# RWKV chunk recurrence, four slots: left half of the Gram product copied by ScalarE, level-one dx in another bank, k copies moved, one output unit loaded in halves

## Chip, cores and metric

The kernel runs on one core of a Trainium2 chip. The metric is device time in microseconds, median of the runs. Of a profiled execution the span is given, from its first instruction to its last.

## What is computed

Two transformer stacks after each other, in float32, for 256 tokens of width 1024: a short convolution mixer, an RWKV-7 mixer, a sparse attention, a forgetting attention, and an MLP of width 4096 behind each of them. Only the recurrence of the RWKV mixer is touched:

```python
def frame_step(state, inp):
    r_t, w_t, k_t, v_t, a_t, b_t = inp
    sa = jnp.einsum('bhvk,bhk->bhv', state, a_t)
    state = (state * w_t[:, :, None, :]
             + sa[..., None] * b_t[:, :, None, :]
             + v_t[..., None] * k_t[:, :, None, :])
    y_t = jnp.einsum('bhvk,bhk->bhv', state, r_t)
    return state, y_t
```

It runs over 256 tokens for 16 heads of 64. In the mixer it is followed by a group norm, a bonus term r*k*v, a gate, and the output projection `rw_w_o`.

## The kernel before

**Chunks and slots.** The 256 tokens are cut in 4 chunks of 64, and the 16 heads in 4 slots of 4 heads (two tiles of 128 rows, each with 2 heads; these two are the halves q = 0 and 1). In a chunk the recurrence is solved by matrices: the Gram product of b with (a, r) gives a strictly triangular 64x64 matrix, whose inverse I - N is built by doubling, in levels 0 to 5. The name for the inverse is `inv_t`, for its transpose `inv_x`. From the inverse, a chain over the 4 chunks gives right-hand side, u, the state and y.

**Steps.** A list, written out by hand, holds the steps of a slot in an order that all engines follow: gram 0, gram 1, tok 0, tok 1, then for each level 1 to 5: t1 0, t1 1, dx 0, dx 1. Between them stand the chain steps rhs, u, sy of the slot before. In slots 1 to 3 the start is: gram 0, rhs (chunk 0), gram 1, u, sy, tok 0, tok 1, t1 0, t1 1 (level 1), rhs (chunk 1), dx 0, u, dx 1, t1 0 (level 2), sy, t1 1, dx 0, dx 1. An engine runs its part of each step in that order and waits by semaphores.

**TensorE** (line 2642 for all products of 64x64): gram 0 writes b x (a, r) into banks `acc[0]`, `acc[1]` (per chunk 64 columns with a, 64 with r) and v, turned, into `un`; gram 1 writes k x (a, r) into `acc[2]`, `acc[3]`; tok turns b and k into `un`; t1 is `n_m` times `inv_x` into the first half of `acc[q]`; dx is t1 times the inverse into the second half of `acc[2 + q]`. In slot 0 products of the value projection are spread between the steps (line 2252 onwards, tile `side`), in slots 2 and 3 a product for the bonus (line 2618) and one for the variance (line 2627).

**VectorE**, gram q: reads the raw product twice, with the level-0 mask (line 1992, to `inv_t`) and the level-1 mask (1993, to `n_m`), adds the identity (1994), writes the product under both masks to `nb_t` (1995, 512 columns; the left, a, columns serve later levels, the right, r, columns y), and transposes (1996). tok q: `nk_t` from `acc[2 + q]` under both masks (2000). dx q: adds dx to the late columns of `inv_t` (2005) and transposes (2008). u: copies y of the chunk before (1980, 1982). sy: the state (2020, 2022). In slot 0 it also prepares mixer inputs (1882 to 1889).

**ScalarE**: gram q copies v (1281), t1 q copies t1 (1287) and in level 1 also the turned b and k (1290); rhs and u are copied at 1293 and 1301. At tok 1 it makes the two decay exponentials for the next slot (`wkv_build`, 1140 and 1141). In slot 0 it computes inverse norms behind step 0 (1169 to 1174) and splits weights (882) behind step 1.

**GpSimd**: for levels 2 to 5 multiplies the left columns of `nb_t` by the level's mask into `n_m` (line 817). Between levels it builds b and k (`build_bk`) and a and r (`build_ar`) of the next slot, and behind them the gate's products.

**SyncE** loads weight units of 1 MB into four stage buffers. Two of these hold, in the RWKV part, arrays of slot 0 and 2 (`v_tok2`, `inv_t2` in the first 4 KB of a partition, `bk_tok2` in the second), so the load of unit `BESIDE_SLOT[0] + NSTAGE`, the third unit of the output projection, waits until the four y of slot 0 are done (line 633).

## Time and profile before

| | us |
|---|---|
| median of three runs | 1351.57 |
| lowest and highest run | 1350.92, 1353.13 |
| span of the profiled execution | 1350.7 |
| TensorE busy in it | 1303.9 (97%) |
| VectorE busy | 948.4 (70%) |
| ScalarE busy | 701.1 (52%) |
| GpSimd busy | 128.3 (9%) |

The slots run from 427.0 to 527.7 us of the span, a last round of chain steps with rows of the output projection to 552.9. A line of a timeline gives start and duration in us, engine, line, operation, tile written <- tiles read, shapes, how many instructions, and in brackets how long the engine was idle before and what ended that. PE is TensorE, PEld its weight load, DVE VectorE, ACT ScalarE, POOL GpSimd, SPq SyncE's queue. "Issue" is idle time for which the profile shows nothing that was awaited. The instruction queue (q8) brings the engines' instructions in pieces of 16 KB.

### The profile page before, as it was taken

To read this page: it belongs to the slowest core of one execution; us is meant where nothing else is said; L and a number is where in the kernel's file an instruction comes from. 1 tells how busy PE (TensorE), PEld (TensorE's weight loads), DVE (VectorE), ACT (ScalarE), POOL (GpSimd) and SP (SyncE) were. 2 spreads that over 40 slices of the span, in tenths; PEclk is the share of its full clock that TensorE was granted. 3 is DMA by queue.
4 is the path that set the end of the run, shared out by engine and by line. 5 is a ranking of instruction groups with operands and counts; after the bars stand their busy time and mean duration, and the time that the engine had idled before them with its cause. 6 is when DMAs were issued, how large, how long until landed. Compare 5 with 4: busy or idle time off the path is not lost. (4 is left out here: it accounts for less than half of the span.)

```text
span 1350.7 us, 24951 instructions
## 1 busy us (share of the span) xinstructions
PE 1303.9 (97%) x10507; PEld 1130.7 (84%) x10507; DVE 948.4 (70%) x1433; ACT 701.1 (52%) x1211; POOL 128.3 (9%) x133
## 2 busy tenths in 40 slices
PE   4999999999999999999999999999999999999997
PEld 2998888997899887788888887888888998888886
DVE  1887788976768776685556888666657677756655
ACT  2534544434467455564444648654445566644443
POOL 0000000010200864100000142000000021000000
PEclk9999999999999999999999999999999999999999
DMA  9997899995341012356665532465565544565561
GB/s 363 373 366 236 302 350 381 356 344 161 110 156 64 4 35 97 98 178 196 188 192 177 176 121 74 150 203 192 187 196 160 170 143 126 172 188 192 183 197 51
DMA packets 177559, 256.90 MB, mean 190 GB/s; under 512 B 10472, under 2 KB 122536, under 8 KB 177448
## 3 DMA queue, kind: packets, MB, share of 16 engines
q1 hardware_dynamic: 177448, 255.31, 57.0%
q8 instruction: 83, 1.36, 0.4%
q14 instruction: 28, 0.23, 0.0%
HBM read 254.25 MB, written 1.05 MB: 189 GB/s over the span
## 5 line engine op out<-in xcount | busy, mean ns | idle before, releaser
L1507 DVE TENSOR_TENSOR w_lo<-stage,w_hi 128x1024 fp32r<-128x1024 f32 (+1 forms) x372 | 447.3, 1238 | 160.4 <-ACT w_hi L882 160.0
L882 ACT ACTIVATE w_hi<-stage 128x1024 fp32r<-128x1024 f32 (+1 forms) x378 | 379.9, 1049 | 211.7 <-PE acc L2311 191.9
L2309 PE MATMUL acc<-w_hi,z_hi 128*128 128x512 f32 x640 | 252.7, 395 | 1.6 <-DVE z_lo L1956 1.6
L2311 PE MATMUL acc<-w_hi,z_lo 128*128 128x512 f32 x640 | 249.4, 390 | 0.0
L2310 PE MATMUL acc<-w_lo,z_hi 128*128 128x512 f32 x640 | 249.2, 389 | 0.0
L2252 PE MATMUL un<-h_both,w_hi 128*128 128x256 f32 x736 | 214.9, 292 | 1.8 <-POOL w_lo L853 1.1
L2253 PE MATMUL un<-h_both,w_hi 128*128 128x256 f32 x736 | 208.8, 284 | 0.0
L2254 PE MATMUL un<-h_both,w_lo 128*128 128x256 f32 x736 | 208.8, 284 | 0.0
L2252 PEld LDWEIGHTS un<-h_both,w_hi 128*128 128x128 f32 x736 | 141.6, 192 | 9.5 <-issue 5.4
L2309 PEld LDWEIGHTS acc<-w_hi,z_hi 128*128 128x128 f32 x640 | 120.1, 188 | 27.8 <-issue 3.9
L2253 PEld LDWEIGHTS un<-h_both,w_hi 128*128 128x128 f32 x736 | 141.7, 193 | 1.2 <-issue 0.7
L2254 PEld LDWEIGHTS un<-h_both,w_lo 128*128 128x128 f32 x736 | 141.7, 193 | 0.0
L2311 PEld LDWEIGHTS acc<-w_hi,z_lo 128*128 128x128 f32 x640 | 120.1, 188 | 25.4
L2310 PEld LDWEIGHTS acc<-w_lo,z_hi 128*128 128x128 f32 x640 | 120.2, 188 | 23.4
L2290 PE MATMUL un<-h_both,w_hi 128*128 128x512 f32 x384 | 121.2, 397 | 0.4 <-DVE w_lo L1507 0.4
L2290 PE MATMUL side<-h_both,w_hi 128*128 128x512 f32 x384 | 120.8, 396 | 0.4
L2293 PEld LDWEIGHTS side<-h_both,w_lo 128*128 128x128 f32 x384 | 72.1, 188 | 17.0
L2293 PEld LDWEIGHTS un<-h_both,w_lo 128*128 128x128 f32 x384 | 72.1, 188 | 16.9
L2293 PE MATMUL un<-h_both,w_lo 128*128 128x256 f32 x384 | 75.5, 278 | 0.0
L2293 PE MATMUL side<-h_both,w_lo 128*128 128x256 f32 x384 | 75.5, 278 | 0.0
L1789 DVE SCALAR_TENSOR_TENSOR ada_sum<-ada_buf,small,ada_sum 128x1024 f32<-128x1024 f32 x49 | 62.8, 1282 | 1.0
L2290 PEld LDWEIGHTS un<-h_both,w_hi 128*128 128x128 f32 x384 | 59.1, 189 | 1.7 <-DVE w_lo L1507 0.6
(393 smaller groups left out, 1885.1 us busy)
## 6 DMA issues: line engine op xcount, KB each, us to landing
stage<-in_mlp_w SPq DMA_DIRECT2D x64, 1024.0 KB
ada_buf<-in_ada_w SPq DMA_DIRECT2D x48, 1024.0 KB, 11.1
stage<-in_w_up SPq DMA_DIRECT2D x32, 1024.0 KB
stage<-in_w_down SPq DMA_DIRECT2D x32, 1024.0 KB
stage<-in_conv_w_in SPq DMA_DIRECT2D x12, 1024.0 KB
stage<-in_rw_w_rkv SPq DMA_DIRECT2D x12, 1024.0 KB
stage<-in_w_in_a SPq DMA_DIRECT2D x8, 1024.0 KB
stage<-in_w_kv_b SPq DMA_DIRECT2D x8, 1024.0 KB
```

Source lines behind the costliest of these rows:

```text
L882: A_(w_hi[u % 2][:, half, 0:n], stage[u % NSTAGE][:, half, 0:n], ACT.Copy).then_inc(hi_made, 1)
L1507: V.tensor_tensor(w_lo[u % 2][:, half, 0:n], stage[u % NSTAGE][:, half, 0:n], w_hi[u % 2][:, half, 0:n].bitcast(F32), ALU.subtract).then_i ...
L1789: V.scalar_tensor_tensor(out=to[:], in0=rows, scalar=by, in1=to[:], op0=ALU.mult, op1=ALU.add).then_inc(ada_weighed, 1)
L2252: MM(out, hi_l, hi_r, start=start, stop=False, skip_group_check=True)
L2253: MM(out, hi_l, lo_r, start=False, stop=False, skip_group_check=True)
L2254: return MM(out, lo_l, hi_r, start=False, stop=stop, skip_group_check=True)
L2290: MM(pair[:, m, :, :], wh[:, kt, c], h_both[:, kt, :, :], start=(kt == 0), stop=False, skip_group_check=True)
L2293: ins = MM(pair[:, m, 0, :], wl[:, kt, c], h_hi[:, kt, :], start=False, stop=(kt == KT - 1), skip_group_check=True)
L2309: MM(y, z_hi[:, kt, q], wh[:, i, :], start=(first and kt == 0), stop=False, skip_group_check=True)
L2310: MM(y, z_hi[:, kt, q], wl[:, i, :], start=False, stop=False, skip_group_check=True)
L2311: ins = MM(y, z_lo[:, kt, q], wh[:, i, :], start=False, stop=(last and kt == KT - 1), skip_group_check=True)
```

## The change

SyncE loads the third unit of the output projection as two halves: the first when it loaded the whole, the second when two more y are done. ScalarE's gram steps copy the left columns of the raw Gram product into `nb_t`, unmasked, first those of `acc[1]`, then, when VectorE has read `acc[0]`, those of `acc[0]`; the two copies of v come behind the second. VectorE masks the right columns only, and waits ahead of that for both copies. GpSimd's level-2 multiplication waits for the copies, and not for VectorE's transpose; in slots 1 and 2 its builds for the next slot come one level later. ScalarE's exponentials move from tok 1 to behind t1 1 of level 1. VectorE's masked copies of the k product move from tok to behind dx of level 1; dx of level 1 goes into the second half of `acc[q]`, and the wait for the k copy goes to dx of level 2. The other edits renumber semaphores, since ScalarE signals five times a slot where it signalled four times.

```diff
--- before.py
+++ after.py
@@ -633,6 +633,13 @@
                     sp.wait_ge(sem("y_done"), CHUNKS)
                 if u == BESIDE_SLOT[1] + NSTAGE:
                     sp.wait_ge(sem("y_done"), CHUNKS * 3)
+                if u == BESIDE_SLOT[0] + NSTAGE:
+                    (_, _, src), = units[u]
+                    for half in range(2):
+                        if half:
+                            sp.wait_ge(sem("y_done"), CHUNKS + 2)
+                        sp.dma_start(stage_wide[u % NSTAGE][:, 2 * half:2 * half + 2, :], src[:, 2 * half:2 * half + 2, :]).then_inc(landed[u % NSTAGE], 16)
+                    return
                 for lo, hi, src in units[u]:
                     sp.dma_start(stage_wide[u % NSTAGE] if u in wide else stage[u % NSTAGE][:, :, lo:hi], src).then_inc(landed[u % NSTAGE], 32 // len(units[u]))
 
@@ -811,14 +818,14 @@
                 for j in WKV_LEVELS[1:]:
                     for q in range(2):
                         if j == 2:
-                            pool.wait_ge(inv_ready, 12 * s + q + 1)
+                            pool.wait_ge(tok_out, 5 * s + 2)
                         else:
                             pool.wait_ge(t1_done, 10 * s + 2 * (j - 3) + q + 1)
                         G.tensor_tensor(n_m[(j - 1) % 2][:, q, :, :], nb_t[s % 2][:, q, :, 0:CHUNK],
                                         level_t[:, j, :].unsqueeze(1).to_broadcast([P, CHUNKS, CHUNK]), ALU.mult).then_inc(nm_ready, 1)
-                    if j == (2 if s else 4) and s + 1 < SLOTS:
+                    if j == (3 if s else 4) and s + 1 < SLOTS:
                         build_bk(s + 1)
-                    if j == (3 if s else 5) and s + 1 < SLOTS:
+                    if j == (4 if s else 5) and s + 1 < SLOTS:
                         build_ar(s + 1)
                     if j == 4 and s >= 2:
                         group_weigh(s - 2)
@@ -1276,18 +1283,25 @@
             for slot in range(SLOTS + 1):
                 for n, (step, s, j, q) in enumerate(wkv_steps(slot)):
                     if step == "gram":
-                        act.wait_ge(v_done, s + 1)
-                        act.wait_ge(lo_made, 2 * (BESIDE_SLOT[0] + 1))
-                        A_(v_tok[SLOT_SET[s]][:, q, :, :], half_bank(un[q], 1), ACT.Copy).then_inc(tok_out, 1)
-                    elif step == "tok":
-                        if q == 1 and s + 1 < SLOTS:
-                            wkv_build(s + 1)
+                        if q == 0:
+                            act.wait_ge(g_done, s + 1)
+                            act.wait_ge(lo_made, 2 * (BESIDE_SLOT[0] + 1))
+                        else:
+                            act.wait_ge(lak_ready, 3 * s + 1)
+                        A_(nb_t[s % 2][:, 1 - q, :, 0:CHUNK], bank4(acc[1 - q])[:, :, 0:CHUNK], ACT.Copy).then_inc(tok_out, 1)
+                        if q:
+                            act.wait_ge(v_done, s + 1)
+                            for m in range(2):
+                                ins = A_(v_tok[SLOT_SET[s]][:, m, :, :], half_bank(un[m], 1), ACT.Copy)
+                            ins.then_inc(tok_out, 1)
                     elif step == "t1":
                         act.wait_ge(t1_done, 10 * s + 2 * (j - 1) + q + 1)
                         A_(t1[:, q, :, :], half_bank(acc[q], 0), ACT.Copy).then_inc(t1_out, 1)
                         if j == 1:
                             act.wait_ge(tok_done, s + 1)
                             A_(bk_tok[SLOT_SET[s]][:, q, :, :, :].rearrange("p b c s -> p (b c s)"), flat(un[q]), ACT.Copy).then_inc(tok_out, 1)
+                            if q == 1 and s + 1 < SLOTS:
+                                wkv_build(s + 1)
                     elif step == "rhs":
                         act.wait_ge(rhs_done, CHUNKS * s + j + 1)
                         A_(wkv_rhs[:], two_pairs(stat_ps), ACT.Copy).then_inc(rhs_out, 1)
@@ -1988,25 +2002,32 @@
                     if step == "gram":
 
                         dve.wait_ge(g_done, s + 1)
+                        if q:
+                            dve.wait_ge(tok_out, 5 * s + 1)
                         raw_n = acc[q][:, :, :].rearrange("p a s -> p (a s)").rearrange("p (c q) -> p c q", c=CHUNKS)
                         V.tensor_tensor(xt, raw_n[:, :, 0:CHUNK], bc4(level_t[:, 0, :], CHUNKS), ALU.mult)
-                        link(V.tensor_tensor(n_m[0][:, q, :, :], raw_n[:, :, 0:CHUNK], bc4(level_t[:, 1, :], CHUNKS), ALU.mult))
+                        ins = V.tensor_tensor(n_m[0][:, q, :, :], raw_n[:, :, 0:CHUNK], bc4(level_t[:, 1, :], CHUNKS), ALU.mult)
+                        if q == 0:
+                            ins.then_inc(lak_ready, 1)
+                            dve.wait_ge(lak_ready, 3 * s + 1)
+                        else:
+                            link(ins)
                         V.tensor_tensor(xt, xt, bc4(eye, CHUNKS), ALU.add)
-                        link(V.tensor_tensor(nb_t[s % 2][:, q, :, :], raw_n, bc4(c_("masks"), CHUNKS), ALU.mult))
+                        dve.wait_ge(tok_out, 5 * s + 2)
+                        link(V.tensor_tensor(nb_t[s % 2][:, q, :, CHUNK:2 * CHUNK], raw_n[:, :, CHUNK:2 * CHUNK], bc4(c_("masks")[:, CHUNK:2 * CHUNK], CHUNKS), ALU.mult))
                         V.transpose(in_line(xn), in_line(xt)).then_inc(inv_ready, 1)
-                    elif step == "tok":
-
-                        dve.wait_ge(gk_done, s + 1)
-                        V.tensor_tensor(nk_t[s % 2][:, q, :, :], bank4(acc[2 + q]), bc4(c_("masks"), CHUNKS), ALU.mult).then_inc(lak_ready, 1)
                     elif step == "dx":
 
                         dve.wait_ge(dx_done, 10 * s + 2 * (j - 1) + q + 1)
                         x_ = late(in_line(xt), j)
-                        ins = V.tensor_tensor(x_, late(flat(acc[2 + q])[:, 2 * P:4 * P], j), x_, ALU.add)
+                        ins = V.tensor_tensor(x_, late(flat(acc[q if j == 1 else 2 + q])[:, 2 * P:4 * P], j), x_, ALU.add)
                         if j < WKV_LEVELS[-1]:
                             link(ins)
                             ins = V.transpose(in_line(xn), in_line(xt))
                         ins.then_inc(inv_ready, 1)
+                        if j == 1:
+                            dve.wait_ge(gk_done, s + 1)
+                            V.tensor_tensor(nk_t[s % 2][:, q, :, :], bank4(acc[2 + q]), bc4(c_("masks"), CHUNKS), ALU.mult).then_inc(lak_ready, 1)
                     elif step == "sy":
                         c = j
                         if c < CHUNKS - 1:
...
                     elif step == "dx":
-                        if j == 1:
-                            pe.wait_ge(lak_ready, 2 * s + q + 1)
+                        if j == 2:
+                            pe.wait_ge(lak_ready, 3 * s + q + 2)
                         pe.wait_ge(t1_out, 10 * s + 2 * (j - 1) + q + 1)
                         for c in range(CHUNKS):
-                            ins = by_head(late(half_bank(acc[2 + q], 1)[:, c, :], j), t1[:, q, c, :], late(xt[:, c, :], j))
+                            ins = by_head(late(half_bank(acc[q if j == 1 else 2 + q], 1)[:, c, :], j), t1[:, q, c, :], late(xt[:, c, :], j))
                         ins.then_inc(dx_done, 1)
...
```

## Rows read from the trace of the kernel before

**Rows 1.** Stretches: us, busy (instructions) of PE, PEld, DVE, ACT, POOL; clock, DMA, GB/s.

```profile
...
426.96:455.02 28.06, 27.36 (x574) 25.25 (x574) 23.39 (x43) 17.53 (x36) 14.09 (x14) 1.00 0.01 3
455.02:478.26 23.24, 21.05 (x712) 19.96 (x709) 18.32 (x51) 12.21 (x33) 18.38 (x19) 1.00 0.03 5
478.26:503.07 24.81, 22.76 (x722) 21.31 (x719) 18.67 (x52) 14.43 (x38) 14.18 (x15) 1.00 0.12 46
503.07:527.69 24.62, 22.73 (x721) 21.23 (x717) 19.40 (x55) 12.75 (x35) 13.42 (x15) 1.00 0.05 10
...
```

**Rows 2.** Waits, 426 to 553 us: total, times, longest.

```profile
...
PE acc L2642 <- DVE inv_x L1996: 2.5, 3, 1.5
...
PE un L2642 <- issue: 1.5, 1, 1.5
...
```

**Rows 3.** Timeline, TensorE, slot 1: start, duration, line, operation [idle before <- releaser].

```profile
...
462.18 0.68 PE L2642 MATMUL acc<-inv_x,n_m 64*64 64x64 f32 x16 [1.50 <-DVE inv_x L1996]
...
464.01 0.45 PE L2642 MATMUL side<-wkv_rhs,inv_t 64*64 64x64 f32 x8
...
465.46 0.45 PE L2642 MATMUL side<-v_tok,bk_tok 64*64 64x64 f32 x8
...
```

**Rows 4.** Timeline, TensorE, slots 2 and 3.

```profile
...
483.92 0.40 PE L2642 MATMUL un<-const,b_fm 64*64 64x64 f32 x12 [1.51 <-issue]
...
485.50 0.22 PE L2642 MATMUL side<-v_tok,nk_t 64*64 64x64 f32 x1
...
487.02 1.13 PE L2618 MATMUL un<-rw,const 128*128 128x256 f32 x4
...
509.49 0.68 PE L2642 MATMUL acc<-inv_x,n_m 64*64 64x64 f32 x16 [0.80 <-DVE inv_x L1996]
...
```

**Rows 5.** Timeline, TensorE, slot 0.

```profile
...
439.44 1.15 PE L2642 MATMUL acc<-inv_x,n_m 64*64 64x64 f32 x32
...
449.69 1.34 PE L2642 MATMUL acc<-inv_x,n_m 64*64 64x64 f32 x32 [0.42 <-DVE inv_x L2008]
...
```

**Rows 6.** DMA by queue, 467 to 475 us: packets, MB, share.

```profile
...
q8 instruction: 3, 0.05, 2.6%
...
```

**Rows 7.** DMA by queue, 481 to 482 us.

```profile
...
q8 instruction: 1, 0.02, 6.2%
...
```

**Rows 8.** DMA in 40 slices of 475 to 481 us.

```profile
...
GB/s 0 0 0 0 0 0 0 0 0 0 0 0 0 0 0 0 0 0 0 68 27 14 82 41 14 164 410 396 396 410 423 396 396 423 437 396 396 410 423 396
...
```

**Rows 9.** Timeline, VectorE, slot 2.

```profile
...
479.86 0.41 DVE L1993 TENSOR_TENSOR n_m<-acc,const 128x256 f32<-128x256 f32 x1
480.31 0.42 DVE L1994 TENSOR_TENSOR inv_t<-inv_t,const 128x256 f32<-128x256 f32 x1
480.65 0.68 DVE L1995 TENSOR_TENSOR nb_t<-acc,const 128x512 f32<-128x512 f32 x1
481.37 0.45 DVE L1996 STREAM_TRANSPOSE inv_x<-inv_t 128x256 f32<-128x256 f32 x1
...
484.26 1.28 DVE L2000 TENSOR_TENSOR nk_t<-acc,const 128x512 f32<-128x512 f32 x2
...
```

**Rows 10.** Timeline, VectorE, slot 3.

```profile
...
505.04 1.13 DVE L1994 TENSOR_TENSOR inv_t<-inv_t,const 128x256 f32<-128x256 f32 x1
...
```

**Rows 11.** Timeline, ScalarE, slot 0.

```profile
...
430.86 1.08 ACT L1174 ACTIVATE ka_mix<-rw,small,vecT 128x256 f32<-128x256 f32 x2
...
```

**Rows 12.** Timeline, VectorE, slot 1.

```profile
...
464.05 0.29 DVE L2005 TENSOR_TENSOR inv_t<-acc,inv_t 128x128 f32<-128x128 f32 x1 [0.37 <-PE acc L2642]
...
464.95 0.46 DVE L1982 COPY tmp<-side 64x64 f32<-64x64 f32 x2
...
```

**Rows 13.** Timeline, VectorE, slot 0.

```profile
...
444.89 0.29 DVE L2005 TENSOR_TENSOR inv_t<-acc,inv_t 128x128 f32<-128x128 f32 x1 [0.67 <-PE acc L2642]
...
```

**Rows 14.** Timeline, ScalarE, slot 1.

```profile
...
458.23 0.62 ACT L1140 ACTIVATE w_cum<-rw 128x512 f32<-128x512 f32 x1
...
463.67 0.28 ACT L1293 ACTIVATE wkv_rhs<-side 128x128 f32<-128x128 f32 x1
...
```

More of the change, by code:

```diff
@@ L2613, in group_step @@
                     if j < 2:
-                        pe.wait_ge(tok_out, 4 * (j + 2) + 4)
+                        pe.wait_ge(tok_out, 5 * (j + 2) + 5)
                     pe.wait_ge(bonus_ready, j)
@@ L2621, in group_step @@
                 if j < 2:
-                    pe.wait_ge(tok_out, 4 * (j + 2) + 3)
+                    pe.wait_ge(tok_out, 5 * (j + 2) + 4)
                 if j:
@@ L2661, in _ @@
                                 pe.wait_ge(t1_out, 10 * s)
-                            pe.wait_ge(tok_out, 4 * s)
+                            pe.wait_ge(tok_out, 5 * s)
                             if s == SLOTS - 1:
@@ L2683, in _ @@
                         if q == 0:
-                            pe.wait_ge(tok_out, 4 * s + 2)
+                            pe.wait_ge(tok_out, 5 * s + 3)
                         for c in range(CHUNKS):
@@ L2711, in _ @@
                                 pe.wait_ge(inv_ready, 12 * s + 12)
-                                pe.wait_ge(tok_out, 4 * s + 4)
-                                pe.wait_ge(lak_ready, 2 * s + 2)
+                                pe.wait_ge(tok_out, 5 * s + 5)
+                                pe.wait_ge(lak_ready, 3 * s + 3)
                                 pe.wait_ge(un_free, freed(V_RKV + 11))
```

## The prediction, made before the changed kernel had run

> **What bounds the kernel now.** I read the table of stretches first. The part that the change touches is the RWKV recurrence, four slots of 28.06, 23.24, 24.81 and 24.62 us [rows 1], and TensorE is busy for 91 to 98% of each. So almost no gain is to be had by making another engine cheaper: what can be won is the sum of TensorE's idle pieces. The table of who waited for whom, for the slots and the output projection behind them, says what those are [rows 2]: 2.5 us in three waits for the transposed inverse of the Gram step (VectorE's line 1996), one of them 1.5 us, and 1.5 us in one piece of "issue", in which nothing in the program was awaited. Behind the slots TensorE runs on almost without a gap into projection and MLP, so that what a slot gains or loses arrives at the end one for one.
>
> Next the timelines. In slot 1 the second half's first product (t1, level 1) starts after 1.50 us of idle, at 462.18 [rows 3]: VectorE makes five operations for each of the two halves, one after the other, and both halves and the next chain step hang on it. In slot 3 the same wait shows as 0.80 us at 509.49 [rows 4]. In slot 2 it is hidden behind the "issue" hole at 482.4 to 483.92 [rows 4]. In slot 0 TensorE has the value projection to do and comes to that product only at 439.44 [rows 5], long after VectorE.
>
> The hole has a neighbour in the DMA view. From 467 to 475 us three 16 KB fetches of the instruction queue went out, some 3.6 us apart [rows 6]. The next one is in 481 to 482 [rows 7], in the last part of the 1 MB load of an output unit, which is issued when the fourth y of slot 0 is done and runs at full rate from 478.7 to about 481.5 [rows 8]. TensorE then ran dry until 483.92.
>
> **The Gram step on VectorE.** Before, one half costs: two reads of the raw product (the second 0.45 from start to start, with its wait), the addition of the identity 0.34, the mask over all 512 columns 0.72 to the transpose, and the transpose itself [rows 9]. The change halves the mask; the 256-column read beside it lasts 0.41, or 0.45 with its wait, so 0.27 is saved for a half, 0.54 for a slot, and not the whole 0.68, since the masked right part stays. Two new waits eat of it. ScalarE copies the left part, and may read a bank only while VectorE does not; in the first half VectorE waits for a copy that starts once it has read twice. A copy of 256 columns from PSUM takes ScalarE what its copy of v takes, which I put at 0.38 by the same shape; VectorE's identity addition of 0.34 hides most of it. In slot 1 I leave 0.1 over. In slot 2 ScalarE's copy of the first right-hand side comes before it in its queue, and I leave 0.25. In slot 3 VectorE's addition is itself stretched to 1.13 [rows 10], which covers the copy wholly. So the second t1 comes earlier by 0.45 (slot 1), 0.3 (slot 2) and 0.5 (slot 3).
>
> In slot 0 the order on ScalarE is bad: behind its first copy stand three passes and two more activations of the inverse norms, whose last begin at 430.86 and end at 431.94 [rows 11]. The second copy comes after them, so VectorE waits from about 429.3 to 432.3 and ends its Gram step near 435 instead of 432.7. I cost this at nothing: the product that needs it starts at 439.44 [rows 5], which leaves more than 4 us. If that cover were gone it would be 2.5 us.
>
> **The masked copies of the k Gram, moved.** Two of them take 1.28 in slot 2 [rows 9]. They stood before the first dx; there VectorE has been idle afterwards (0.37 in slot 1 [rows 12]), so they hid. Now one stands behind each dx of level 1, in front of the copies of y, the next dx and the state. Slot by slot, each 0.64:
> Slot 1: dx of the first half would be read at about 463.6 instead of 464.05, its transpose ends at 464.25, then comes the k copy until 464.9 and the copies of y until 465.6. Before, the first of y's last two copies began at 464.95 [rows 12], ended by 465.4, and TensorE's step began at 465.46 [rows 3] directly behind it. So that step is now at about 465.75: the 0.45 won turns into 0.3 lost.
> Slots 2 and 3: the bonus product of 1.13 us [rows 4] stands in TensorE's queue between the first dx and the step that wants y, so the copies have room and the gain stays.
> Slot 0: VectorE goes on with mixer work after each dx, and reads the level-2 dx at 444.89 after 0.67 of idle [rows 13]. 1.28 more, less 0.67, is 0.6 late, and TensorE, which waited 0.42 for just this chain at 449.69 [rows 5], waits 0.6 more. VectorE has no idle time between the two. I take +0.6; bounds 0 and +1.28.
>
> **The decay exponentials on ScalarE, moved.** Two activations of 0.62 [rows 14] now come behind the second copy of b and k, right in front of the copy of the second right-hand side (463.67 in slot 1), for which TensorE's next step at 464.01 waits [rows 3, 14]. In slot 1 that step comes at about 464.45 (0.45 late); VectorE's k copy above runs in the same time, so the two delays overlap and slot 1 stays at +0.3; bounds -0.45 (none of it bites) and +0.6. In slot 2 the bonus product again covers it but for 0.1. In slot 0 ScalarE has idle time there. Slot 3 has none to make.
>
> **GpSimd.** Its level-2 multiplications no longer wait for VectorE's transpose and start about 1 us earlier in slots 1 and 2; the build of b and k for the next slot goes behind level 3, and that of a and r behind level 4. Level 3 can be multiplied as soon as the second t1 is over. The queue then stands waiting for the exponentials until about 464.3, and the build ends 1.5 us later than now, but the next slot starts at 478.26 [rows 1], and level 4 is multiplied by 468.3, wanted near 472. Nothing on the path.
> What can cost is that two engines meet: VectorE's addition of the identity took 0.42 in slot 2, with GpSimd idle, and 1.13 in slot 3, with GpSimd at work on the gate [rows 9, 10], and the level-2 multiplications now fall on just such VectorE operations. I take +0.1 for all slots, bounds 0 and 0.7 (1.13 less 0.42) for each of three slots. The Trainium skill, SBUF — State Buffer, section "SBUF: two separate sides", says that a VectorE operation with two SBUF inputs and a GpSimd operation that reads SBUF exclude each other for the whole instruction. By that rule the stretch would be up to one GpSimd operation for each meeting; the row of slot 3 agrees, 0.71 longer; the sum by it would be 2.1 instead of 0.1 at most.
>
> **Level one's dx in its own bank.** Same 32 products, another address. It lets dx start without the k copy. TensorE didn't wait for that copy in any slot: its queue order set the start. Worth 0, and the waits at level 2 are long met (the first k copy of slot 1 ends at 464.9, that dx is after 466).
>
> **The output unit in halves.** SyncE issues 0.5 MB when it issued 1 MB, and 0.5 MB when two more y are done, in slot 2 near 492. Nobody wants the unit before the projection, 55 us later, and the queue's next load waits for y of slot 3 anyway. So it costs nothing. At the rate shown, some 400 GB/s from 478.7 [rows 8], the first half is through at about 480.1 instead of 481.5. If the fetch, due near 478.4, has waited for the load, it comes 1.4 us earlier, about the length of the hole, 1.51 us [rows 4]. I take the hole as gone. VectorE is then the one that is late: its Gram step ended near 483.9, a state update before the k copies at 484.26 [rows 9], and would end at 483.6, the second t1 is through by 484.2 and the next chain product begins there instead of at 485.50: -1.3; the bonus product, at 487.02 [rows 4] because it waited for ScalarE's copies of b and k, brings 0.2 more and ScalarE's exponentials cost 0.1: slot 2 -1.4, bounds 0 (hole stays) and -1.8. The second half could delay a fetch near 493 to 495 by at most its own 1.4 us; a delay of some 3 us made a hole of 1.5, so this one should make at most 0.3, which is inside the bounds.
>
> **Sum.** Slot 0 +0.6, slot 1 +0.3, slot 2 -1.4, slot 3 -0.5, meetings +0.1: -0.9 us. The profiled span is 1350.7, so 1349.8; the median of the three timed runs, 1351.57, lies 0.87 over that span, so 1350.7 us.
>
> **Rivals.** *The hole stays*, because the fetch and the load are neighbours and not cause and effect. For it: no row shows the fetch waiting, only that it is late. Against: the three fetches before it keep their distance, and it comes with the load's end. Slot 2 then gives 0 and the sum is +0.5: 1352.1 us. The Trainium skill, DMA: Bandwidth & Descriptors, section "Queues, rings and completion order", speaks for this rival: each DMA engine takes turns between queues packet by packet, so a fetch would be held up by one packet and not by a megabyte. By that rule the time would be this rival's; the trace so far disagrees, with a fetch that came only in the load's last microsecond.
> *All of it is cover*: the k copies and exponentials fall into idle time in slots 0 and 1 too. Slot 0 at 0, slot 1 -0.45, slot 2 -1.7, slot 3 -0.5: -2.65, 1348.9 us. For it: VectorE is busy only 75 to 83% of each slot [rows 1]. Against: the idle time is not in front of the two steps named.
> *VectorE becomes the bound* (the slower side): after level 1 both halves alternate through VectorE, and the 1.28 us of k copies come out on the path in each of four slots, 5.1 in all, from the point at which VectorE's idle time before the level-2 dx (0.67 in slot 0, about 0.35 in the others) is less than the copies. Less 1.2 of Gram gains, less 1.0 for the hole with the old rest: +2.9, 1354.5 us. Against: bonus products in slots 2 and 3 give VectorE 0.5 to 0.9 of idle just there.
>
> **How the numbers follow.** Forecast 0.60, hole stays 0.18, all cover 0.14, VectorE the bound 0.05, else 0.03. A measurement of this kernel can tell about 0.2%, 2.7 us, from no change: below 1348.9 is faster, above 1354.3 slower. Forecast and hole-stays lie well inside; half of all-cover, and some of the scatter of the forecast (the runs of before span 2.2 us), goes to faster: 0.14. VectorE-the-bound and scatter give slower 0.07, and 0.79 is left. The range takes in both neighbours and the scatter around them: 1348.3 to 1353.6.
>
> **What would show it.** Right: no "issue" idle of TensorE near 482; an instruction fetch between 479 and 480.5; slot 2 shorter by 1.2 to 1.6, slot 3 by 0.5, slot 1 longer by 0.3 with TensorE waiting for the copies of y (line 1982's place) instead of the transpose, slot 0 longer by 0.6 with a wait near 450. Wrong: a hole of 1 us or more anywhere in slots 1 to 3, slot 0 unchanged, or VectorE additions of 1 us in slots 1 and 2.

## The result and the profile after

The changed kernel takes 1353.9 us, median of 14 runs (1353.25 to 1355.35), where the kernel before, on the same chip, takes 1351.49 (14 runs, 1350.65 to 1354.65). The ratio is 1.0017, 95% interval 1.0010 to 1.0024: 2.4 us slower, just under the 0.2% that I had set as what can be told, with an interval that leaves no change out. The forecast was 1350.7, with a range up to 1353.6: a gain of 0.8 us where 2.4 were lost, wrong by 3.2 and 0.3 above the range.

The table of stretches, cut at the Gram starts of the kernel after, answers to [rows 1]. The last stretch runs here to the first row of the output projection; the same stretch of before is the first line.

```profile
...
503.07:532.49 29.42, 27.35 (x792) 24.78 (x789) 21.44 (x59) 15.35 (x42) 18.14 (x19) 1.00 0.21 69
...
```

```profile
...
427.44:456.62 29.18, 27.87 (x573) 25.55 (x574) 24.55 (x43) 18.14 (x38) 15.18 (x15) 1.00 0.01 3
456.62:480.87 24.25, 20.85 (x713) 19.85 (x709) 18.59 (x52) 12.88 (x35) 16.76 (x18) 1.00 0.02 4
480.87:505.51 24.64, 22.92 (x720) 21.28 (x718) 18.94 (x52) 15.04 (x40) 14.14 (x15) 1.00 0.15 46
505.51:534.70 29.19, 27.41 (x795) 24.86 (x791) 20.93 (x59) 16.06 (x44) 18.10 (x19) 1.00 0.21 70
...
```

The second number of a line is its length. Against 28.06, 23.24, 24.81 and 29.42 that is +1.12, +1.01, -0.17 and -0.23: +1.73 us in the slots. Another 0.48 us lies before them (the first Gram product starts at 427.44, not at 426.96), where no instruction was changed. That is not the change's: in the profiles of the experiments below this start lies anywhere from 426.86 to 429.44, and at 426.86 and 426.87 in e3 and e4, which differ from the kernel after only behind it. So 1.73 us is what the change did in the slots; the rest of the 2.4 is of the size by which runs of one kernel differ.

The table of who waited for whom shows how the idle time of TensorE has changed hands. [Rows 2] had 2.5 us in three waits for the transposed inverse of the Gram step and 1.5 in a single piece of "issue". Of after, the rows for TensorE and the longest new ones of others:

```profile
...
PE acc L2663 <- DVE inv_x L2026: 2.6, 7, 0.7
DVE nb_t L2017 <- ACT nb_t L1291: 2.4, 1, 2.4
...
ACT nb_t L1291 <- DVE n_m L2009: 1.5, 1, 1.5
...
PE side L2663 <- ACT wkv_u L1315: 1.4, 1, 1.4
...
PE side L2663 <- ACT wkv_rhs L1307: 1.2, 2, 1.0
```

Line 2026 is the transpose behind a dx (2008 of before): TensorE now waits for that seven times, 2.6 us. It waits 1.4 and 1.2 us for ScalarE's copies of u and of the right-hand side, for which the same table of before has no row. The big old waits are gone; new ones stand at other producers. The timeline of TensorE after, the pieces of it that answer to [rows 3 to 5]: two in slot 0, three in slot 1, three in slot 2 (the middle one is the chain product of [rows 4], without idle time) and one in slot 3.

```profile
...
447.39 1.34 PE L2663 MATMUL acc<-inv_x,n_m 64*64 64x64 f32 x32 [0.63 <-DVE inv_x L2026]
...
451.30 0.93 PE L2663 MATMUL acc<-inv_x,n_m 64*64 64x64 f32 x18 [0.54 <-DVE inv_x L2026]
...
461.48 0.39 PE L2663 MATMUL side<-wkv_u,bk_tok 64*64 64x64 f32 x6 [1.39 <-ACT wkv_u L1315]
...
463.61 0.68 PE L2663 MATMUL acc<-inv_x,n_m 64*64 64x64 f32 x16 [0.29 <-DVE inv_x L2018]
...
466.47 0.45 PE L2663 MATMUL side<-wkv_rhs,inv_t 64*64 64x64 f32 x8 [1.03 <-ACT wkv_rhs L1307]
...
485.22 0.40 PE L2663 MATMUL un<-const,b_fm 64*64 64x64 f32 x12 [0.26 <-issue]
...
486.81 0.22 PE L2663 MATMUL side<-v_tok,nk_t 64*64 64x64 f32 x1
...
499.40 0.68 PE L2663 MATMUL acc<-inv_x,n_m 64*64 64x64 f32 x16 [0.72 <-DVE inv_x L2026]
...
511.71 0.68 PE L2663 MATMUL acc<-inv_x,n_m 64*64 64x64 f32 x16 [0.40 <-DVE inv_x L2018]
...
```

**Slot 1** shows the exchange best. The second t1, which had waited 1.50 [rows 3], starts at 463.61: 6.99 us behind the slot's start, before 7.16. So 0.17 is won where 0.45 was forecast. The rest of that wait has moved in front of the u step at 461.48. ScalarE's timeline says why:

```profile
...
460.32 0.38 ACT L1291 ACTIVATE nb_t<-acc 128x256 f32<-128x256 f32 x1 [1.49 <-DVE n_m L2009]
460.60 0.66 ACT L1295 ACTIVATE v_tok<-un 128x256 f32<-128x256 f32 x2
461.13 0.30 ACT L1315 ACTIVATE wkv_u<-side 128x128 f32<-128x128 f32 x1
...
464.62 0.59 ACT L1302 ACTIVATE bk_tok<-un 128x512 f32<-128x512 f32 x1
465.10 0.63 ACT L1147 ACTIVATE w_cum<-rw 128x512 f32<-128x512 f32 x1
465.62 0.63 ACT L1148 ACTIVATE w_inv<-rw 128x512 f32<-128x512 f32 x1
466.14 0.28 ACT L1307 ACTIVATE wkv_rhs<-side 128x128 f32<-128x128 f32 x1
...
```

The second copy of a left half may start only when VectorE has read that bank twice; ScalarE stands 1.49 us for it, and behind it in its queue are the two copies of v and the copy of u that TensorE wants. Then the exponentials, 465.10 to 466.2, stand in front of the copy of the right-hand side, and TensorE waits 1.03. That step comes 9.85 us behind the slot's start; before it was 464.01 - 455.02 = 8.99 [rows 3]. It is 0.86 late against the kernel before, not 0.45.

**Slot 2.** The "issue" piece is 0.26 instead of 1.51 [rows 4], and the next chain product starts at 486.81, 5.94 behind the slot's start, where it was 485.50 - 478.26 = 7.24: 1.30 earlier, as forecast. But at the slot's end only 0.17 of that is left. The fences show VectorE's split of an output unit in slot 2 (its product w_lo, the rest of a weight), before and then after, and GpSimd beside it in the kernel after.

```profile
...
494.75 1.30 DVE L1507 TENSOR_TENSOR w_lo<-stage,w_hi 128x1024 fp32r<-128x1024 f32 x1 [0.33 <-ACT w_hi L882]
...
```

```profile
...
496.33 2.21 DVE L1521 TENSOR_TENSOR w_lo<-stage,w_hi 128x1024 fp32r<-128x1024 f32 x1 [0.32 <-ACT w_hi L889]
...
```

```profile
...
496.19 1.27 POOL L801 TENSOR_TENSOR rw<-tmp,rw 128x512 f32<-128x512 f32 x1 [0.15 <-POOL ar L783]
497.42 2.39 POOL L824 TENSOR_TENSOR n_m<-nb_t,const 128x256 f32<-128x256 f32 x2
...
```

GpSimd's weighing of a group runs 496.19 to 497.46 and VectorE's split is issued 0.14 us after its start. The split ends at 498.54, which is the end of the weighing and 1.1 us more: it looks as if it had waited for it. GpSimd's next two multiplications, issued at 497.42, take 2.39 us, and 1.42 elsewhere (440.70), as if they in turn had waited for the split. The next inverse is late by it, and TensorE waits 0.72 at 499.40. Before, the weighing was at 492.95, through before the split began.

**Slot 0.** VectorE's timeline after, first the wait of 2.36 us for the second left copy, which I had foreseen (about 3 us), then what stands behind the level-one dx; below it the same three mixer lines of before.

```profile
...
432.25 0.42 DVE L2017 TENSOR_TENSOR nb_t<-acc,const 128x256 f32<-128x256 f32 x1 [2.36 <-ACT nb_t L1291]
...
443.81 0.65 DVE L2030 TENSOR_TENSOR nk_t<-acc,const 128x512 f32<-128x512 f32 x1
444.38 1.01 DVE L1896 TENSOR_TENSOR tmp<-tmp,ss_inv 128x512 f32<-128x512 f32 x1
445.43 1.10 DVE L1897 SCALAR_TENSOR_TENSOR tmp<-tmp 128x512 f32<-128x512 f32 x1
446.56 0.29 DVE L2023 TENSOR_TENSOR inv_t<-acc,inv_t 128x128 f32<-128x128 f32 x1
...
447.91 1.52 DVE L1899 SCALAR_TENSOR_TENSOR rw<-rw,tmp 128x512 f32<-128x512 f32 x1
...
```

```profile
...
442.85 0.65 DVE L1882 TENSOR_TENSOR tmp<-tmp,ss_inv 128x512 f32<-128x512 f32 x1
443.53 0.69 DVE L1883 SCALAR_TENSOR_TENSOR tmp<-tmp 128x512 f32<-128x512 f32 x1
...
446.24 1.04 DVE L1885 SCALAR_TENSOR_TENSOR rw<-rw,tmp 128x512 f32<-128x512 f32 x1
...
```

The k copies don't only take their own 1.2 us. They push the mixer operations from 442.85 to 444.38, which is 1.05 us later behind the slot's start, where GpSimd is at work from 444.12 on, and the three lines take 3.63 instead of 2.38.

### The profile page after: what moved, and what is told of

Same layout as the page of the kernel before. It is cut to its first block and busy times, and to the rows that moved or that the text cites. A ratio compares the mean times of both kernels' runs of the same rounds, so it can differ in the third digit from the quotient of the medians.

```text
span 1351.8 us, 24960 instructions
## 1 busy us (share of the span) xinstructions
PE 1303.7 (96%) x10507; PEld 1130.7 (84%) x10507; DVE 949.7 (70%) x1433; ACT 703.6 (52%) x1219; POOL 127.7 (9%) x133
## 3 DMA queue, kind: packets, MB, share of 16 engines
HBM read 254.25 MB, written 1.05 MB: 189 GB/s over the span
```

## The experiments

Lengths are us from Gram start to Gram start, the fourth to the first projection row; "sum" also has the 20.4 us of the projection's rows, which are the same in all. They are the fine measure here, since the scatter of whole runs is as large as what is looked for. A median is of 11 runs, or of as many as stand in brackets behind it. The intervals are of the ratio to the kernel before on the same chip.

| kernel | slot 0 | 1 | 2 | 3 | sum | median | ratio, 95% |
|---|---|---|---|---|---|---|---|
| before | 28.06 | 23.24 | 24.81 | 29.42 | 125.92 | | 1 |
| after | 29.18 | 24.25 | 24.64 | 29.19 | 127.64 | 1353.9 (14) | 1.0010 to 1.0024 |
| e1: before, halves | 28.08 | 23.26 | 23.75 | 29.46 | 124.93 | 1350.7 (11) | 0.9977 to 0.9995 |
| e2: after, whole load | 29.19 | 24.24 | 25.76 | 29.18 | 128.75 | 1354.96 | 1.0013 to 1.0030 |
| e3: after, exponentials back | 29.19 | 23.91 | 24.20 | 29.19 | 126.88 | 1353.8 | 1.0000 to 1.0017 |
| e4: after, builds back | 29.20 | 24.24 | 23.89 | 29.19 | 126.91 | 1353.93 | 1.0003 to 1.0020 |
| e5: after, k copies back | 28.55 | 23.92 | 24.39 | 29.18 | 126.42 | 1352.43 | 1.0000 to 1.0017 |
| e6: all three back | 28.54 | 22.82 | 23.13 | 29.29 | 124.19 | 1350.39 (11) | 0.9977 to 0.9995 |
| e7: e1, k copies moved | 29.18 | 25.38 | 24.43 | 29.46 | 128.82 | 1353.24 | 1.0003 to 1.0021 |
| e8: e1, builds later | 28.04 | 23.75 | 24.32 | 29.46 | 125.94 | 1351.97 | 0.9995 to 1.0013 |
| e9: e6, norms later | 28.00 | 22.82 | 23.54 | 29.14 | 123.88 | 1349.7 (11) | 0.9977 to 0.9995 |
| e10: after, norms later | 29.19 | 24.24 | 24.40 | 29.19 | 127.41 | 1353.88 (10) | 1.0008 to 1.0027 |
| e11: after, weighing cut | 29.20 | 24.23 | 23.77 | 29.19 | 126.77 | 1354.03 (1) | |

**The load in halves, alone and left out.** e1 is the kernel before with only this edit; e2 is the kernel after without it.

```diff
+                if u == BESIDE_SLOT[0] + NSTAGE:
+                    (_, _, src), = units[u]
+                    for half in range(2):
+                        if half:
+                            sp.wait_ge(sem("y_done"), CHUNKS + 2)
+                        sp.dma_start(stage_wide[u % NSTAGE][:, 2 * half:2 * half + 2, :], src[:, 2 * half:2 * half + 2, :]).then_inc(landed[u % NSTAGE], 16)
+                    return
```

> The kernel before with the output unit loaded in halves and nothing else. If the fetch waited for the load: TensorE's issue hole in slot 2 goes from 1.5 us to 0.3 or less, slot 2 goes from 24.8 to about 23.8 us (VectorE's Gram step is next in line there), the total to 1.0 us below before. If fetch and load are only neighbours: hole and total as before.

> The changed kernel with the output unit loaded whole again. If the fetch waited for the load: a hole of 1.5 us in slot 2 and the slot 1.0 to 1.3 us longer than in the changed kernel (24.64). If not: no difference to the changed kernel.

Measured: slot 2 falls by 1.06 in e1 and rises by 1.12 in e2, and no other slot moves. TensorE's timeline, e1 and then e2:

```profile
...
484.52 0.40 PE L2649 MATMUL un<-const,b_fm 64*64 64x64 f32 x12 [0.33 <-issue]
...
```

```profile
...
486.15 0.40 PE L2656 MATMUL un<-const,b_fm 64*64 64x64 f32 x12 [1.37 <-issue]
...
```

And the DMA view, 40 slices and the queue's row: e1, in 482 to 483 us, and e2, in 483 to 484 us. The slice of 655 GB/s in the first, and that of 984 in the second, hold the fetch.

```profile
...
GB/s 82 0 0 0 655 0 0 0 0 0 0 0 0 0 0 0 0 0 0 0 0 0 0 0 0 0 0 0 0 0 0 0 0 0 0 0 0 0 0 0
...
q8 instruction: 1, 0.02, 5.7%
...
```

```profile
...
GB/s 164 410 492 410 246 573 410 246 573 492 82 655 573 82 573 573 164 410 492 410 164 573 410 164 492 410 0 984 328 0 0 164 0 0 0 0 0 0 0 0
...
q8 instruction: 1, 0.02, 6.3%
...
```

In all four kernels the fetch comes with the last bytes of the load that is under way, or up to 0.2 us behind them: at 481.35 and 483.68 behind the whole megabyte (before, e2), at 482.10 and 482.68 behind the half (e1, after). The fetch ahead of it, at about 477.4 in after and 477.3 in e2, is through before the load moves in both. Behind the slot's start that is 3.1 and 3.0 us with the whole load, 2.0 and 1.8 with the half, and the product that ends TensorE's idle piece starts 2.4 to 2.6 us behind the fetch in each of the four. So the load is the cause of the hole, in both kernels, and the rival that they are only neighbours falls. The fetch still waits for the half load; it only has less to wait for. The halves alone are worth 1.0 to 1.1 us.

**Each moved step taken back by itself.** e3 puts ScalarE's exponentials back at the second tok step, e4 GpSimd's two builds back one level, e5 VectorE's k copies back at tok (the dx of level one stays in its own bank in all).

```diff
+                    elif step == "tok":
+                        if q == 1 and s + 1 < SLOTS:
+                            wkv_build(s + 1)
...
-                            if q == 1 and s + 1 < SLOTS:
-                                wkv_build(s + 1)
```

```diff
-                    if j == (3 if s else 4) and s + 1 < SLOTS:
+                    if j == (2 if s else 4) and s + 1 < SLOTS:
                         build_bk(s + 1)
-                    if j == (4 if s else 5) and s + 1 < SLOTS:
+                    if j == (3 if s else 5) and s + 1 < SLOTS:
                         build_ar(s + 1)
```

```diff
+                    elif step == "tok":
+                        dve.wait_ge(gk_done, s + 1)
+                        V.tensor_tensor(nk_t[s % 2][:, q, :, :], bank4(acc[2 + q]), bc4(c_("masks"), CHUNKS), ALU.mult).then_inc(lak_ready, 1)
...
-                        if j == 1:
-                            dve.wait_ge(gk_done, s + 1)
-                            V.tensor_tensor(nk_t[s % 2][:, q, :, :], bank4(acc[2 + q]), bc4(c_("masks"), CHUNKS), ALU.mult).then_inc(lak_ready, 1)
```

> The changed kernel with ScalarE's two decay exponentials back at the tok step. If the queue on ScalarE is the cause of the loss: TensorE's wait of 1.03 us for the copied right-hand side in slot 1 goes, slot 1 goes from 24.25 to about 23.3 us, slot 2 by 0.2, the total by 1.0 to 1.2. If the meetings of GpSimd and VectorE are the cause, GpSimd's builds come 1.3 us earlier and what they meet changes: slot 1 gains less than 0.5 net.

> The changed kernel with GpSimd's builds of b, k and of a, r back behind levels 2 and 3 in slots 1 and 2. If meetings of GpSimd and VectorE are the cause: VectorE's weight split in slot 2 takes 1.3 instead of 2.2 us and slot 2 shortens by 0.9, the split in slot 1 by 0.4, slot 0 stays at 29.2. If ScalarE's queue is the cause: no more than 0.2 in all, and GpSimd now stands waiting for the exponentials with level 3 queued behind it, which would cost a few tenths.

> The changed kernel with VectorE's masked copies of the k product back at the tok step. If the moved k copies make slot 0 longer, by pushing VectorE's mixer work among GpSimd's multiplications: slot 0 from 29.2 back to 28.1 us, VectorE's five mixer operations of level 2 to 4 together from 6.0 back to about 4.7. If the wait of 2.4 us for ScalarE's left copy in slot 0 is what costs: slot 0 stays at 29.2. Slot 1 changes by less than 0.3 either way, since ScalarE's queue holds TensorE there.

Measured: 0.76, 0.73 and 1.22 us come back, 2.71 if added, in different slots: the exponentials in slots 1 and 2 (0.34, 0.44), the builds in slot 2 alone (0.75), the k copies in slot 0 (0.63), slot 1 (0.33) and slot 2 (0.25). Three expectations were missed. The exponentials were expected to give back 0.95 in slot 1. The builds were expected to shorten VectorE's split in slot 1 by 0.4, but it takes 1.64 us in e4 and 1.66 in after, and that slot doesn't move. The k copies were expected to bring slot 0 back to 28.1; it comes to 28.55, and e9 below shows what holds the rest. Their 0.33 in slot 1 is a meeting too: VectorE's split at the slot's start takes 1.76 us in after and 1.44 in e5, and the second t1 comes 6.99 and 6.67 behind the slot's start. In e3 TensorE's wait for the right-hand side in slot 1 is gone, and the wait that lay under it comes out, for the copies of y that now stand behind a k copy:

```profile
...
466.91 0.45 PE L2664 MATMUL side<-v_tok,bk_tok 64*64 64x64 f32 x8 [0.50 <-DVE tmp L1997]
...
```

That is the wait which the forecast gave slot 1, and it shows that two of the moved steps were late for the same TensorE step, one hidden under the other.

**All three back.** e6 has all three edits at once: what is left of the change are the left copies by ScalarE, the Gram order on VectorE, GpSimd's earlier level-2 multiplication, level one's dx in its own bank and the halves.

> The changed kernel with k copies, exponentials and GpSimd's builds all where they were: what is left of the change is the left copy by ScalarE, level one's dx in its own bank, the earlier level-2 multiplication and the load in halves. If moved work is the cause of the loss and the Gram part is sound: slots of 28.1, 22.9, 23.4 and 29.1 (to the first output row), total 1.8 to 2.2 below before. If the left copy itself costs (waits between ScalarE and VectorE): slots 0 and 1 at or above 28.1 and 23.2, total no better than the load in halves alone (1.0 below before by slots).

Measured: 3.45 us less than after, 0.74 more than the three single steps, so they covered for each other. Slots 1 and 2 are the shortest yet, 0.42 and 1.68 under before. The time is 1350.39, ratio 0.9986. The Gram part of the change is sound by the slots: beyond e1 it brings 0.44 in slot 1, 0.62 in slot 2 and 0.17 in slot 3, and costs 0.46 in slot 0 (where 28.1 us had been expected).

**Moved alone.** e7 is e1 with the k copies moved and the dx of level one in its own bank, without ScalarE's copies; e8 is e1 with the builds one level later (the reverse of e4's diff).

> The kernel before, with the load in halves, level one's dx in its own bank and the k copies behind dx; nothing of the Gram part, exponentials or builds. If the moved k copies cost by VectorE's order: slot 0 28.7 to 29.2 instead of 28.08, slot 1 23.9 to 24.1 instead of 23.26 (the copies of y come 0.65 later and TensorE waits for them), slot 2 and 3 unchanged within 0.2. If they only cost together with the other moves: all slots within 0.2 of the load in halves alone.

> The kernel before, with the load in halves, and GpSimd's builds in slots 1 and 2 one level later; nothing else. If meetings of GpSimd and VectorE cost: VectorE's weight split in slot 2 goes from 1.5 to 2.0 us or more and the slot grows by 0.4 to 0.8 over 23.75, slot 1 within 0.4. If GpSimd's order is off the path: slots unchanged within 0.1.

Measured: in e7 slot 0 takes 29.18, which is after's 29.18, so the k copies alone are enough for slot 0's loss, 1.10 us. (Taking them back in e5 returned only 0.63, since the late left copy then comes out from under them.) Slot 2 loses 0.68, where nothing had been expected: TensorE's piece of "issue" there is 0.96 us and in e1 0.33, so that most of the loss is the hole come back, with the load in halves, and not shown to be the k copies'. Slot 1 loses 2.1, but there the granted clock was 0.72 in the mean of 465 to 471 us, and about 1.2 of it is that (below). In e8 the builds cost 0.49 in slot 1 and 0.57 in slot 2, with nothing else changed. VectorE's split took 1.25 and 1.52 us in the two slots of e1; in e8:

```profile
...
470.00 1.80 DVE L1514 TENSOR_TENSOR w_lo<-stage,w_hi 128x1024 fp32r<-128x1024 f32 x1 [0.32 <-ACT w_hi L889]
...
494.07 2.03 DVE L1514 TENSOR_TENSOR w_lo<-stage,w_hi 128x1024 fp32r<-128x1024 f32 x1 [0.33 <-ACT w_hi L889]
...
```

So the loss goes with the stretch of that one operation: 0.55 and 0.51 longer, 0.49 and 0.57 lost.

**The meeting by itself.** e11 is the kernel after, in which GpSimd's weighing of the first normalised group works on 8 of the 256 columns of each block. It leaves the rest of that product out and keeps its signals.

```diff
-                G.tensor_tensor(rw_k[:, t, :], y_wkv[:, t, :], rw_k[:, t, :], ALU.mult).then_inc(weighed, 1)
+                w = 8 if j == 0 else SEQ
+                G.tensor_tensor(rw_k[:, t, 0:w], y_wkv[:, t, 0:w], rw_k[:, t, 0:w], ALU.mult).then_inc(weighed, 1)
```

> The kernel after, with GpSimd's first weighing of a normalised group cut from 256 columns of each block to 8 (its work left out there, its signals kept). Theory (GpSimd's operations on the shared memory stretch VectorE's split of output weights in slot 2, 2.21 us where it takes 1.30 alone): the split starts at 496.3 as before and takes 1.9 us or less, TensorE's wait for inv_x behind it falls from 0.72 to 0.4 us or less and slot 2 from 24.64 to 24.3. Rival (the split takes 2.2 us because of ScalarE or the arriving load beside it): it stays at 2.2, and so do the wait and the slot.

VectorE and GpSimd in slot 2 of e11:

```profile
...
497.75 1.23 DVE L1522 TENSOR_TENSOR w_lo<-stage,w_hi 128x1024 fp32r<-128x1024 f32 x1 [0.33 <-ACT w_hi L890]
...
```

```profile
...
497.62 0.22 POOL L802 TENSOR_TENSOR rw<-tmp,rw 128x16 f32<-128x16 f32 x1 [0.15 <-POOL ar L783]
497.80 2.46 POOL L825 TENSOR_TENSOR n_m<-nb_t,const 128x256 f32<-128x256 f32 x2
...
```

The split takes 1.23, TensorE's wait for the inverse behind it is gone, and slot 2 falls to 23.77, by 0.87. That is more than expected (24.3), as the split was expected at 1.9 or less. GpSimd's next two multiplications take 2.46 here and 2.39 in after, where 1.42 is usual: they meet the split in both kernels, and on GpSimd it costs the slot nothing. The two engines don't slow each other down by a part; the one that comes second waits until the other's operation is over. In after, 1.13 us of the weighing was left when the split was issued, and the split took 0.98 longer. ScalarE and the arriving load were the same in both kernels, so they are not the cause.

**The inverse norms behind the second left copy.** VectorE's 2.36 us of waiting in slot 0 come from ScalarE's order. e9 is e6, e10 is after, with this edit:

```diff
-                    if n == 0:
+                    if n == 1:
                         inverse_norms(2)
-                    if n == 1:
                         split(U_RWV + 3)
                         inverse_norms(3)
```

> The kernel with the three moves taken back (k copies, exponentials, GpSimd's builds), and in slot 0 ScalarE's third group of inverse norms behind the second copy of the left halves in place of ahead of it. Theory (VectorE's wait of 2.36 us for that copy is what is left of slot 0's loss): the copy comes at about 428.6, the wait falls under 0.3 us, the mixer's five operations start 2 us earlier and the first dx with them; slot 0 falls from 28.54 to about 28.05 us, slots 1 to 3 stay at 22.8, 23.1 and 29.3, the four slots and the projection together come to 123.7 us, 2.2 us below the kernel before, and the ratio to about 0.998. Rival (slot 0's rest is the level-one dx itself or the left copies' place on TensorE's side): slot 0 stays at 28.5, ratio 0.9985 as without this edit.

> The kernel after with that one edit: the third group of inverse norms behind the second left copy. Theory (in slot 0 the k copies behind dx push the mixer into GpSimd's builds, whatever comes ahead of them): VectorE's wait of 2.36 us goes, but it then only waits longer for TensorE's level-one dx; slot 0 comes to between 28.7 and 29.2 us, as the mixer's first operations may start earlier while the k copies keep their place. Rival (the wait for the left copy was the whole loss): slot 0 at 28.1 and the time at about 1352.8 us. The other slots as in the kernel after: 24.25, 24.6 and 29.2.

Measured in e9: no wait at VectorE's masked copy, 429.66 instead of 431.78, and slot 0 at 28.00, 0.54 under e6. So with the three moves taken back the copy's place cost half a microsecond, which I had put at nothing. In e10 that wait is gone too, but slot 0 stays at 29.19: VectorE is idle 1.77 us for TensorE's first dx (1.17 in after), and behind it the k copies send the mixer into GpSimd's operations as before. The rival (the wait was the whole loss) falls. Slot 2 of e9 is 0.41 longer than in e6, with an "issue" piece of 0.29 us at the place of the old hole; how well the fetch fits differs from kernel to kernel by some tenths.

e9 is the best version found: 2.04 us under before by the slots, 1349.7 us in the median of 11 runs, where before had 1352.12 on that chip; ratio 0.9986 (0.9977 to 0.9995). By the time alone it can't be told from e6 or e1.

## Why the prediction was wrong

The forecast's terms add up to -0.9 us, and the slots gave +1.73: 2.6 too much, 0.5 of it in slot 0, 0.7 in slot 1, 1.2 in slot 2 and 0.3 in slot 3, less the 0.1 for meetings. Most of it is two terms: the meetings of VectorE and GpSimd, and the queues behind the moved steps.

- **What bounds the kernel** (TensorE's idle pieces, one for one to the end): right. In all thirteen kernels TensorE's waits moved with the slots, and the projection behind took 20.37 to 20.41.
- **The hole** (slot 2 -1.4, gone with the halves): right in cause and nearly in size. e1 and e2 give 1.06 and 1.12; the chain product came 1.30 earlier, as written. The fetch came 1.81 behind the slot's start, which on the clock of before is 480.07, between the 479 and 480.5 foretold; it waited for the half load as it had for the whole, also as written. Of the hole 0.26 stayed. The second half did no harm: no "issue" piece stands beside it.
- **Meetings of VectorE and GpSimd** (+0.1, bounds 0 and 2.1): the main failure, and a term that was mis-sized within its bounds. In slot 2 one meeting gave back 0.87 (e11), more than half of what this slot missed; in slots 1 and 2 of e8 they cost 0.49 and 0.57; in slot 0 they are the part of the loss above the copies' own time. I looked at the level-2 multiplications, for which nothing met, and not at what moving the builds does to the rest of GpSimd's queue: a build moved behind the next level brings the weighing of slot 2, at j = 4, directly behind a build, onto VectorE's split. For GpSimd I wrote "nothing on the path", which was true of its own results and not of the memory that it holds. The row for it was there: 0.42 against 1.13 [rows 9, 10]. The Trainium skill, SBUF — State Buffer, section "SBUF: two separate sides", says that a VectorE operation with two SBUF inputs and a GpSimd operation that reads SBUF exclude each other for a whole instruction. The runs agree: 2.21 against 1.23 for the split, and 2.46 against 1.42 for GpSimd when it came second.
- **Slot 0** (+0.6 for the k copies, 0 for the late left copy): +1.12. The copies cost 1.10 alone (e7): about the 1.28 less 0.67 of idle that I counted, and the stretched mixer operations on top. The left copy at nothing was wrong too, as e9 shows (0.54), though not in the changed kernel itself, where the k copies hide it (e10). I took the cover from the product that needs VectorE's transpose; the queue behind it on VectorE, the mixer, had no such cover.
- **Slot 1** (+0.3): +1.01. The wait for the copies of y was right in kind (0.50 in e3). Mis-sized were the exponentials: the right-hand side comes 8.81 us behind the slot's start in e3 and 9.85 in after, so they hold it up by 1.04 and not 0.45. By the rows the reason is ScalarE's queue: its second left copy stands 1.49 us for VectorE with the copy of u behind it, the first t1 comes 6.07 behind the slot's start instead of 4.98, right ahead of the second, and both halves' copies and the exponentials then stand in one unbroken row in front of the right-hand side. The wait for u alone loses nothing: in e6 it is still 1.07, and slot 1 is shorter than before. I had named what the new wait costs VectorE and not what it holds up on ScalarE, its own queue.
- **Slot 2, the rest; slot 3** (-0.5): slot 3 gave -0.23, with the second t1 at 6.20 behind the start instead of 6.42. The eye addition is as long as before there. The exponentials cost 0.44 in slot 2 (e3), where I put 0.1 behind the bonus product.
- **Span to median** (+0.87): the profiled run of the kernel after was 1353.57 with a span of 1351.8, that is 1.8 around the span. Had I taken that for before, its profiled run would have been one of 1352.5, one of the slower ones of that kernel, with a stretch of lower clock that costs about 1.5 us (below). The two errors nearly cancel, by luck, so this step did little harm: the sum was wrong by its other terms.
- **Before the slots**: the 0.48 us of untouched work is the scatter of single profiles (426.86 to 429.44 in the thirteen), and no term of the forecast.

Of the rivals, "VectorE becomes the bound" (1354.5) is nearest in time and has the k copies right. But its 5.1 us did not come: taking the copies back returned 1.22. What held was a sum of three small losses, 3.45 together, which ate a gain of 1.7. That the time lies near this rival's is luck.

## What to carry to other kernels

When a step is moved to an engine's idle time, follow everything that stands behind it in that engine's queue until the next idle piece, and lay the shifted operations beside those of the engine that shares the memory: where a VectorE and a GpSimd operation now fall together, the second waits for what is left of the first, up to the whole of it. Where a change has parts that win and parts that make room for them, run each part alone: here the winning parts were sound, and the steps moved to make room for them cost twice what these won. A piece of "issue" on TensorE that ends with a large load is worth a look at the instruction queue; half a load at a time brought it from 1.5 to 0.3 us in e1, though in e7 it was still 0.96.

## What the runs showed of the hardware

- **VectorE and GpSimd exclude each other per instruction** on such operations: 1.23 us with GpSimd's weighing cut to 0.22, 2.21 when issued 0.14 us behind a weighing of 1.27 (e11, after).
- **An instruction fetch waits for a load**: it came with the last bytes of the load of 1 MB, 6.4 to 6.5 us behind the fetch ahead of it, where the fetches until then had stood 3.5 to 4.7 apart (before, e2), and the hole it made was 1.4 to 1.5 us; with half a load it came at the end of the half, 5.1 to 5.3 us behind the one ahead, and the hole was 0.3 (e1, after). The Trainium skill, DMA: Bandwidth & Descriptors, section "Queues, rings and completion order", says an engine takes turns between queues packet by packet; these traces don't show that. Why is open: only the size of the load was varied.
- **The clock can fall after a short idle piece, and need not.** In e7 TensorE had been idle for 0.53 and 1.50 us in slot 1, and behind them its granted clock was at the lower level (1.2 GHz) until just before 469.98; 16 products took 0.92 us that take 0.68 elsewhere. The eight groups of products from 466.07 on took 3.91 us, the same eight in e1 2.70 (464.00 to 466.70): 1.2 us lost. In e1 and in before TensorE had been idle at the same two places for 0.2 and 1.50 us, and the clock stayed at the higher level. The first fence is the stretch with its mean clock, the second TensorE's timeline.

```profile
...
465.00:471.00 6.00, 4.56 (x96) 4.43 (x96) 3.17 (x10) 2.69 (x9) 4.90 (x7) 0.72 0.01 3
...
```

```profile
...
466.07 0.92 PE L2648 MATMUL acc<-inv_x,n_m 64*64 64x64 f32 x16 [1.50 <-DVE inv_x L2003]
...
469.98 0.66 PE L2648 MATMUL acc<-inv_x,n_m 64*64 64x64 f32 x16
...
```

  The profiled run of before has such a stretch of lower clock far behind the recurrence (first fence), after has none (second). Idle pieces stand ahead of it in both, 0.57 and 1.06 us in before and 0.58 and 1.05 in after, so they alone don't decide it. From the product behind them to the one at 829.65 before took 15.34 us, and after 13.85 for the same: 1.5 us. That is why after was 2.2 us late at the end of the recurrence and only 1.1 at the end of the span.

```profile
...
800.00:830.00 30.00, 28.09 (x216) 23.06 (x216) 26.43 (x65) 18.30 (x56) 15.35 (x19) 0.94 0.36 120
...
```

```profile
...
800.00:830.00 30.00, 28.30 (x231) 23.77 (x230) 27.16 (x71) 19.71 (x57) 16.95 (x22) 1.00 0.35 112
...
```
